# Low weight halves multiplied last, low-half subtraction in two pieces, and about a hundred steps of a two-block transformer kernel in a new order

## What is computed

```python
def first_block(...):                      # one layer
    h_lat = modulate(x, g1, sh1, sc1); h_ctx = modulate(ctx, g1, csh1, csc1)   # 512 and 256 tokens
    p = h @ w_in                           # z, x/B/C, dt, q, k, v, gates
    y_ssd = rmsnorm((ssd_bidir(silu(conv3(xbc)), dt) + D * xs) * silu(z))      # scan in both directions, chunks of 128
    y_att = softmax(rope(q) @ [k_window | k_ctx | sink]) @ v                   # 16 heads, 4 kv heads
    x = x + gt1 * ((g_ssd * (y_ssd @ w_o_ssd) + g_att * (y_att @ w_o_att)) @ w_out)
    u = conv3(modulate(x, g2, sh2, sc2) @ w_up)
    return rmsnorm(x + gt2 * ((silu(u_a) * u_b) @ w_down))
def second_block(x, mem, ...):
    z = rms_norm(x) @ w_in                 # forgetting attention q,k,v; S5 input u; memory query; gates
    y_fox, y_s5, y_mem = forgetting_attention(...), glu(gelu(s5_ssm(u))), memory_attention(qm, mk, mv)
    x = x + (sum of gates_i * (y_i @ w_proj_i)) @ w_out
    return rms_norm(x)
```

## Time and profile before

| | |
|---|---|
| median of the runs | 2019.16 us |
| the profiled execution's own time | 2017.95 us |
| its span, first to last instruction | 2016.6 us |
| PE matmul busy | 1950.4 us, 97% of the span, 11104 matmuls |
| DVE busy | 1099.8 us, 55% |
| ACT busy | 899.0 us, 45% |
| POOL busy | 825.3 us, 41%, 463 instructions |
| DMA | 242.41 MB, mean 120 GB/s |

### The profile page before, as it was taken

One profiled execution on the slowest core, in us unless ns is written; L12 is line 12 of the kernel. 1 busy time (PEld: TensorE's weight loads), 2 busy tenths in 40 slices (PEclk: granted clock), 3 DMA queues, 4 the chain that ended last, 5 costly groups with the idle time before them and its releaser, 6 DMA issues.

```text
span 2016.6 us, 27939 instructions
## 1 busy us (share of the span) xinstructions
PE 1950.4 (97%) x11104; PEld 1594.7 (79%) x11104; DVE 1099.8 (55%) x1800; ACT 899.0 (45%) x1713; POOL 825.3 (41%) x463
## 2 busy tenths in 40 slices
PE   6989999999999999999999999999999999999998
PEld 4867787878777777888788888888788777888886
DVE  5577868684575656774544440345755566611114
ACT  3465656564455544223443442334655454522222
POOL 1222323222534316464444444444474551654442
PEclk9999999999999999999999999999999999999999
DMA  7245353533322216665333334335222323433331
GB/s 303 74 162 169 110 181 108 186 116 121 94 59 58 58 42 261 228 220 171 102 93 105 93 90 149 97 104 181 64 70 74 86 56 103 156 94 96 95 107 71
DMA packets 92321, 242.41 MB, mean 120 GB/s; under 512 B 28192, under 2 KB 31392, under 8 KB 90784
## 3 DMA queue, kind: packets, MB, share of 16 engines
q1 hardware_dynamic: 88784, 231.98, 36.6%
q10 hardware_dynamic: 3408, 8.65, 1.1%
HBM read 223.14 MB, written 14.29 MB: 118 GB/s over the span
## 4 chain that ended last, share of the span: by engine, by line
PE 64%; DVE 5%; ACT 2%; POOL 1%; DMA 1%; issue 1%; SPq 0%; DVEq 0%; ACTq 0%; POOLq 0%
PE ps L902 17%; PE ps L904 16%; PE ps L903 16%; PE ps L1269 2%; PE ps L1256 1%; PE ps L1244 1%; PE ps L1331 1%; DMA modr<-in_w_mod 1%; PE ps L1350 1%; PE ps L1035 1%; PE ps L1037 1%; PE ps L1036 1%; PE ps L959 1%; DVE ps L2127 1%; PE ps L1311 1%; PE ps L960 1%
## 5 line engine op out<-in xcount | busy, mean ns | idle before, releaser
L2761 POOL TENSOR_TENSOR wlo<-raww,whi 128x1024 fp32r<-128x1024 f32 (+2 forms) x244 | 570.4, 2345 | 825.4 <-ACT whi L1396 824.5
L1396 ACT CAST whi<-raww 128x1024 fp32r<-128x1024 f32 (+2 forms) x279 | 279.2, 1006 | 168.4 <-PE ps L904 155.0
L902 PE MATMUL ps<-hT_h,whi 128*128 128x512 f32 (+1 forms) x688 | 257.4, 374 | 2.3 <-POOL wlo L2761 0.8
L903 PE MATMUL ps<-hT_l,whi 128*128 128x512 f32 (+1 forms) x688 | 250.6, 364 | 0.0
L904 PE MATMUL ps<-hT_h,wlo 128*128 128x512 f32 (+1 forms) x688 | 250.5, 364 | 0.0
L902 PE MATMUL ps<-H_h,whi 128*128 128x512 f32 x480 | 189.0, 394 | 0.7 <-ACT Pf L1431 0.7
L904 PE MATMUL ps<-H_h,wlo 128*128 128x512 f32 x480 | 187.0, 390 | 0.0
L903 PE MATMUL ps<-H_l,whi 128*128 128x512 f32 x480 | 186.9, 389 | 0.0
L902 PEld LDWEIGHTS ps<-hT_h,whi 128*128 128x128 f32 x688 | 130.0, 189 | 26.7 <-issue 4.8
L903 PEld LDWEIGHTS ps<-hT_l,whi 128*128 128x128 f32 x688 | 130.0, 189 | 21.0 <-issue 1.4
L904 PEld LDWEIGHTS ps<-hT_h,wlo 128*128 128x128 f32 x688 | 129.8, 189 | 21.2
(11 more groups left out here) (554 smaller groups left out, 4503.5 us busy)
## 6 DMA issues: line engine op xcount, KB each, us to landing
ec<-csd SPq DMA_DIRECT2D x32, 1024.0 KB, 7.8
raww<-in_w_up SPq DMA_DIRECT2D x44, 512.0 KB, 3.6
modr<-in_w_mod SPq DMA_DIRECT2D x32, 512.0 KB, 5.6
raww<-in_w_xbc SPq DMA_DIRECT2D x24, 512.0 KB, 3.7
raww<-in_w_gl SPq DMA_DIRECT2D x24, 512.0 KB, 3.6
raww<-in_w_z SPq DMA_DIRECT2D x16, 512.0 KB, 3.9
raww<-in_w_g SPq DMA_DIRECT2D x16, 512.0 KB, 3.6
raww<-in_w_os SPq DMA_DIRECT2D x16, 512.0 KB, 4.3
```

Of the source, the lines that this page charges most:

```text
L902: e.matmul(o, whi[:, i, c], hi(k)[:, t0:t1], start=(k == 0), stop=False)
L903: e.matmul(o, whi[:, i, c], lo(k)[:, t0:t1], start=False, stop=False)
L1396: e.copy(o, x.rearrange("p (k c) -> p k c", c=64) if p == plan.first["dt", 0] else x).then_inc(*w_high.mark(("high", p)))
L2761: e.tensor_tensor(o, x, h.bitcast(F32), ALU.subtract).then_inc(*p_wlow.mark(("split", p), ("raw free", p)))
```

## The change

There are four parts.

1. `gemm`, `token_major`, "duo", "o2" and "mv" wait for the high part of the weights first, run the 16 matmuls with `whi`, then wait for the low part and run the 8 matmuls with `wlo`. In `gemm` the low part is waited for in two pieces. Eight tiles whose activations arrive one by one (FRESH) keep the three matmuls of a block together, but have the new waits.
2. POOL makes a low part of 1024 columns in two instructions of 512.
3. The table AHEAD_OF has 131 entries in place of 36. The new ones move steps of the first block, 41 of them in the scan, and of the start of the second block; a few of the second block's are changed.
4. No instruction is removed. Only POOL's subtractions of 1024 columns become two each, and PE has 483 more semaphore waits in its queue (1639 for 1156).

```diff
 AHEAD_OF = [
-    (('mpair', 0), ('ypair5', 5)), (('fpair', 4), ('gs', 3)), (('mpair', 1), ('gs', 2)), (('s5out', 5), ('gs', 0)),
+    (('mpair', 0), ('ypair5', 5)), (('fpair', 4), ('gs', 3)), (('fpair', 1), ('gs', 2)), (('mpair', 1), ('fpair', 1)),
...
+    (('memsq', 7), ('os', 1)), (('memsq', 6), ('piece', 6)), (('reload',), ('qpair', 3)),
...
+FRESH = {("oa", 0), ("os", 0), ("wout", 0), ("down", 0), ("glu", 0), ("proj", 0, 0), ("proj", 1, 0), ("proj", 2, 0)}
...
-                    PE.wait_ge(at("split", p))
+                    PE.wait_ge(at("high", p))
                     for (t0, t1), b in zip(cols, banks):
...
                             e.matmul(o, whi[:, i, c], hi(k)[:, t0:t1], start=(k == 0), stop=False)
                             e.matmul(o, whi[:, i, c], lo(k)[:, t0:t1], start=False, stop=False)
+                            if s in FRESH:
+                                PE.wait_ge(at("split", p))
+                                last = e.matmul(o, wlo[:, i, c], hi(k)[:, t0:t1], start=False, stop=(k == kt - 1))
+                        for k in range(k0, k0 + kk) if s not in FRESH else ():
+                            c = slice((k - k0) * 128, (k - k0 + 1) * 128)
+                            if k in (k0, k0 + 4):
+                                PE.wait_ge(at("first half" if k == k0 else "split", p))
                             last = e.matmul(o, wlo[:, i, c], hi(k)[:, t0:t1], start=False, stop=(k == kt - 1))
...
-                    e.tensor_tensor(o, x, h.bitcast(F32), ALU.subtract).then_inc(*p_wlow.mark(("split", p), ("raw free", p)))
+                    if n == 1024:
+                        e.tensor_tensor(o[:, 0:512], x[:, 0:512], h[:, 0:512].bitcast(F32), ALU.subtract).then_inc(*p_wlow.mark(("first half", p)))
+                        e.tensor_tensor(o[:, 512:1024], x[:, 512:1024], h[:, 512:1024].bitcast(F32), ALU.subtract).then_inc(
+                            *p_wlow.mark(("split", p), ("raw free", p)))
+                        continue
```

More of the change, by code:

```diff
@@ new lines @@
+    (('score', 3, 1), ('pt', 2, 0)), (('score', 2, 2), ('pt', 1, 1)), (('rms', 'y'), ('score', 2, 2)),
+    (('pt', 1, 4), ('rms', 'y')), (('qrot', 2), ('pv', 0)), (('pt', 0, 0), ('q', 3)), (('pt', 0, 3), ('score', 1, 0)),
+    (('kst', 1), ('pt', 0, 3)), (('gate', 1), ('gate', 2)), (('gateout', 2), ('qrot', 1)), (('a2',), ('out', 3, 3)),
+    (('out', 3, 1), ('cap', 3, 2, 1)), (('out', 3, 0), ('cscale', 3, 1, 0)), (('k', 8), ('decay', 3, 0, 0)),
+    (('state', 3, 1, 4), ('k', 8)), (('state', 3, 0, 4), ('zgate', 11)), (('zsum', 9), ('state', 3, 1, 2)),
@@ L1006, in tensor_program @@
                         e.matmul(ps[:, b, :], whi[:, i, c], lo(q), start=False, stop=False)
-                        last = e.matmul(ps[:, b, :], wlo[:, i, c], hi(q), start=False, stop=(q == 7))
+                    for x in two:
+                        p = plan.first[x]
+                        i, b = plan.pair[p] % PAIRS, bank_of((x, 0))
+                        if q == 2:
+                            PE.wait_ge(at("split", p))
+                        for r in {0: (), 1: (), 2: (0, 1, 2)}.get(q, (q,)):
+                            c = slice(r * 128, (r + 1) * 128)
+                            last = e.matmul(ps[:, b, :], wlo[:, i, c], hi(r), start=False, stop=(r == 7))
                         if q == 7:
@@ L1054, in tensor_program @@
                             e.matmul(o, hi(k)[:, t], whi[:, i, w], start=(k == 0), stop=False)
-                            e.matmul(o, hi(k)[:, t], wlo[:, i, w], start=False, stop=False)
-                            last = e.matmul(o, lo(k)[:, t], whi[:, i, w], start=False, stop=(k == 7))
+                            e.matmul(o, lo(k)[:, t], whi[:, i, w], start=False, stop=False)
+                    PE.wait_ge(at("split", p))
+                    for c in (0, 1):
+                        use = ("tm", "w_mv", n, c)
+                        o = ps[:, bank_of(use), 0:256]
+                        t = slice(c * 128, (c + 1) * 128)
+                        for q in range(4):
+                            k, w = 4 * half + q, slice(q * 256, (q + 1) * 256)
+                            last = e.matmul(o, hi(k)[:, t], wlo[:, i, w], start=False, stop=(k == 7))
                         last.then_inc(*gemm_done.mark(*[("gemm", use)] * half, *[("used", p)] * (c == 1)))
```

70 lines of the change are left out of this document (55 added, 15 removed), and 11 rows, old and new, of the table AHEAD_OF.

## The result

The changed kernel takes 2000.9 us (median of 4 runs, 1999.68 to 2001.92), where the kernel before takes 2018.99 us (4 runs). The ratio is 0.9908, with a 95% interval from 0.9891 to 0.9925: it is 0.9% faster, by 18.1 us. The forecast was 2005.0 us, 0.7%, within 1995 to 2016. The profiled execution of the changed kernel took 2001.82 us, 16.1 us less than that of the kernel before (2017.95).

What follows compares the result with a forecast made beforehand. The prediction took PE's matmuls as the bound, with about 42 us of idle time open. Its terms summed to 16.2 us, less 2 us for returning waits: 14.2 us, so 2005.0 us (0.7% faster), range 1995 to 2016 us.

Steps and rivals of the forecast that it cites:

- the case: Whole kernel: the forecast's own case, a gain summed from many small PE waits, 1999 to 2011 us, chance 0.61.
- A: Tiles where PE waits for `wlo`: starting once `whi` is there gains 4.8 us, bounds 0 and 6.3.
- C: Scan's turns and states: moved steps shorten waits for banks and scaled x, gaining 5.0 us, bounds 0.5 and 9.5.
- B: Outputs of the scan's group 0: waits for "keep" to empty bank 5 shrink by 2.0 of 4.4 us.
- E: Entry to attention: ACT empties a bank earlier for the first score, gaining 1.7 us, bounds 0 and 2.5.
- F: Window attention, memory's norm, first "up" tiles, second block: 4 of 22 us in small waits, bounds -2 and 10.
- That gives 2.2 us: Longest `wlo` wait, 2.90 us near 1461 us: PE starts at about 1462.2 instead of 1464.42.
- D: POOL's subtraction in two pieces: DVE is held up less, 0.5 us at some five places in group 0.
- Rival 2: DVE is let through everywhere: halving could clear all PE waits on DVE, 8.4 us more, about 1996.6 us; chance 0.12.
- G: "reload" ahead of five of eight casts on ACT: PE waits inside "oa" 0, costing 1.3 us.
- H: PE's queue: the 483 added semaphore waits cost 0.
- The 2 us for waits that come back: Allowance of 2 us for new waits created by moves, with DVE as the bound in group 0.

Runs made afterwards that it cites:

- e1_low_last: The kernel before with only the new PE loops, low parts multiplied last (old table, POOL's subtraction in one instruction): 2016.31 us, ratio 0.9993.
- e7_whole: The changed kernel with POOL's subtraction in one instruction again: 2001.8 us, ratio 0.9915.
- e3_order: The kernel before with the new table of 131 entries and nothing else: 2003.33 us, ratio 0.9926.
- e8_keep: The kernel before with three moves alone, "keep" of group 0's chunks 0, 1 and 2 ahead of the next chunk's decay weights: 2014.63 us, ratio 0.9984.
- e2_halves: The kernel before with POOL's subtraction in two instructions and nothing else: 2015.24 us, ratio 0.9984.
- e6_waits: The kernel before with 2132 more, already satisfied semaphore waits on PE, ahead of each third matmul in `gemm`: 2018.21 us, ratio 1.0.
- e5_no_reload: The changed kernel with "reload" put back behind the eight casts: 1998.71 us, ratio 0.9897.
- e11_keep_halves: The kernel before with both the three moves of "keep" and POOL's subtraction in two instructions: 2013.97 us, ratio 0.9979.
- e12_attention: The kernel before with only the 30 moves of the entry to attention and the window attention: 2014.38 us, ratio 0.9985.
- e10_both: The changed kernel without "reload"'s move and without the seven early moves of the scan's group 0: 1997.29 us, ratio 0.9897.
- e9_no_early: The changed kernel without the seven moves around the first turns and states of the scan's group 0: 1997.19 us, ratio 0.9895.

## Why the prediction was right, and where it was not

The direction, the range and the case were right: many small waits of PE in 42 us of idle time, each worth 1 or 2 us. The sum of 14.2 us against 16.1 in the traces and 18.1 in the medians hides that its terms were off, in both directions: A and C came out several us too high, B, E and F too low. That the total came so near is in part luck.

*A, low parts last: 4.8 us forecast, 1.4 us measured* (e1_low_last, with an interval from 3.4 us faster to 0.4 us slower). The step that failed is "That gives 2.2 us". The waits for `wlo` did all go, but behind two of the longest stood a second wait that the profile of before doesn't name. For the activations at line 1005 the text had seen this and counted half: nothing came at 961 us, while the 0.65 us at 1343 us went; at 1461 us it had not looked at what ACT did just behind, and 1.1 us came for 2.2. The other short waits went as forecast, and part of the gain was lost to the clock's fall at 533 us. Together with the order the new loops bring at most a little: 0.9915 with them (e7_whole) and 0.9926 without (e3_order), with overlapping intervals.

*B, bank 5: 2.0 us forecast, 3.7 in the trace.* The step by which "keep" ahead of the decay weights "does not by itself help" is refuted by e8_keep. DVE busy for 47.71 of 49 us does bound the stretch as a whole, but PE waits for one particular piece of DVE's work; that the rest, such as the convolution of the next group, has time is the likely reason and was not tested by itself.

*C, turns and states: 5.0 us forecast.* The waits for `xw` came out at 4.8 us, under the 6 of the forecast. At group 3 PE won 2.6 us (399 to 524) and from 187 to 399 us 1.3 us. The first turn and the states of group 0, for which 2.9 us of gain were expected, gave nothing: 0.1 and 0.2 us of loss in e3_order and e7_whole, 1.9 in the changed kernel, whose clock fell there. The net is 2 us in the changed kernel and 3.7 in e3_order. The prediction asked what each moved step wins, and not what the step had covered where it stood. It also misread where the waits for `xw` lie: "Of the other 7.7 us of this kind most lie in group 0", but group 0 has 2.4 us of the 9.5, groups 1 and 2 have 3.3, group 3 has 3.8, and it was in group 3 that they went (0.3 us are left).

*D, the halving: the mechanism was right,* in the size roughly too by itself (2.5 us less 0.7 forecast, 3.3 measured). Between 137 and 187 us it takes from the same wait as B, where the forecast had counted it; its other 2.0 us, from 524 to 748 us, the forecast had not. In the changed kernel the times show nothing of it (e7_whole), PE's idle time at most 2.1 us. DVE's two-input instructions of 1024 columns last 2.3 us at most, where they took up to 3.4, as the sign given for D said. POOL's extra busy time was 46.6 us for 26, since it is now POOL that waits. Rival 2, the rule at its full size, did not happen: e2_halves leaves the waits for `xw` at 9.9 us, and e3_order shortens them just as well without the halving.

*E and F: 5.7 us forecast; 5.3 us from 524 to 748, 2.9 from 787 to 993, 1.0 from 1265 to 1488 and 1.9 up to 1939 in the trace, 11.1 in all,* part of which is A's (the wait of 0.8 us of line 902 and those of line 1005 lie there). This is the term that made the forecast too small. "4 of the 22 us that are spread over small waits" was a guess without rows. From 524 to 748 us the small waits, all but those for `wlo` and ahead of the first score, fell from 3.1 to 1.3 us, and 1.7 us more came out of the busy time. From 1488 to 1939 us idle time fell by 1.6 us. In the changed kernel as a whole small waits are hardly fewer, about 20 us by the prediction's own sum (51.3 us of idle time, less 17.1, 7, 4.8, 1.4 and 1.0), since new ones have come. The first score still waits 0.8 us, so the sign given for E ("no wait over 0.5 us") was missed.

*G, "reload": +1.3 us forecast, +0.55 in the trace.* The wait and its place are right, the size is under half of what was worked out, and the sign given for it, 1 to 2 us inside the product, was missed at 0.45. The step that failed is what it compared with: it let today's product run without a wait, 0.68 us for each block, so that PE would ask for the eighth at 766.7. In the trace of before the eighth starts at 768.39, and the arrival that was forecast for the change, 768.3, is no later than that. Measured from its start, the product's eighth block came 0.40 us later with the change (6.23 for 5.83 us), and its start 0.13 us later.

*H: 0, shown* by e6_waits.

*The 2 us for waits that come back.* Such waits came, but elsewhere than in the group 0 where the text looked for them: 2.3 us at the turns of B, which took the place of others, 1.4 us for `yg` in group 3, 1.4 us for `Pf` at 1447 us, and 1.3 us for "qk" at 1452.

One premise was incomplete. The prediction says that without new matmuls the kernel can win only in PE's idle time. PE's busy time moved as well: 1950.4 us before, 1949.2 with the change, 1945.0 in e3_order, for the same 11104 matmuls. Two things move it: the short waits that hide under the overlap of two matmuls (1.7 us from 524 to 748 us), and the granted clock, which the last section shows.

## What to carry to other kernels

A wait in the profile names its last releaser; before counting its whole length as gain, look at what ends next on the other engines and banks, and take only the difference. Two repairs of one wait are not worth their sum, so each is measured alone and together. When a step is moved to fill a gap, ask what it had covered where it stood: here the moved turns uncovered a wait of 2.3 us, as much as their moves saved. And when two kernels differ by 1 or 2 us, compare PE's idle time stage by stage ahead of the medians: the falls of the clock touch it little.

## What was not expected of the hardware

The granted clock falls to 0.50, which is 1.2 GHz of 2.4, for some 3 or some 7 us at some places, and these differ between traces. In the kernel before one lies behind the wait of 2.90 us at 1461 us. Busy time by stretch of the kernel before (columns as in the earlier trace rows, the clock third from the end):

```profile
1460.00:1464.00 4.00, 1.52 (x6) 0.49 (x4) 2.25 (x3) 2.78 (x5) 3.84 (x6) 1.00 0.01 2
1464.00:1468.00 4.00, 3.58 (x20) 3.61 (x21) 2.55 (x8) 2.63 (x10) 3.84 (x4) 0.67 0.47 132
```

The same place in e6_waits, which has the same order of matmuls and the same wait, 2.89 us, keeps its clock:

```profile
1464.00:1468.00 4.00, 2.19 (x18) 2.22 (x19) 3.41 (x8) 1.90 (x8) 3.84 (x3) 1.00 0.34 86
1468.00:1472.00 4.00, 4.00 (x58) 3.77 (x57) 0.85 (x3) 4.00 (x10) 3.84 (x4) 1.00 0.14 50
```

And in the changed kernel a new one stands behind the wait of 2.30 us at 110 us, and one later where PE was never idle:

```profile
108.00:112.00 4.00, 1.05 (x6) 0.71 (x6) 3.18 (x6) 3.02 (x5) 0.89 (x1) 0.85 0.31 98
112.00:116.00 4.00, 4.00 (x13) 2.37 (x12) 1.01 (x2) 1.19 (x4) 1.89 (x2) 0.50 1.02 355
...
1316.00:1320.00 4.00, 4.00 (x20) 4.00 (x20) 0.67 (x4) 0.00 (x0) 1.59 (x1) 0.50 0.00 0
```

A PE that is busy for 4.00 of 4.00 us here does half as much, so that the busy time grows without a matmul more: four us at 0.50 cost 2 us, nearly as much as the wait ahead of them. But the wait alone does not decide it. The fall near 110 us was there in the traces of the changed kernel and of e5_no_reload, and absent in e3_order and e7_whole, which have the same wait; the one at 1461 us was there in the kernel before, e2_halves and e8_keep, and absent in e6_waits, e11_keep_halves and e12_attention, all with a wait of 2.9 us. What decides stays open. So does what sets off the fall near 1316 us, inside a run of matmuls of 256 columns without a gap: one between 1312 and 1336 us is in every trace of this study. It lasts some 3 us in some and some 7 in others, which makes up to 2 us of difference in any reading of the table behind 1265 us.

The times of whole executions follow the clock too. In the 75 executions of the kernel before that ran beside the experiments, the mean granted clock lies between 0.993 and 0.999 and the time between 2014.0 and 2022.2 us: the 11 with 0.994 took 2020.5 us in the mean, the 14 with 0.997 took 2016.9. That is some 1.2 us for each 0.001. The changed kernel had 0.9955 in the mean of its 4 runs, e5_no_reload 0.9965, e10_both 0.9975 and e9_no_early 0.9978. By these numbers, an estimate, the clock makes 1.2, 2.4 and 2.8 us of the 2.2, 3.6 and 3.7 us by which these three were faster. Whether e9_no_early owes its clock to the missing wait at 110 us or to chance, five runs against four don't tell.
